# A decoder trunk on one core: two of three units in step at the stage entries, low parts moved on VectorE, and a retention end with three open output tiles

## The reference

```
for i in range(4):
    a = rms_norm(h, norm_g[i, 0])
    m = gmlp(a) if i % 3 == 0 else nsa(a) if i % 3 == 1 else retention(a)
    h = h + rms_norm(m, norm_g[i, 1])
    f = (silu(b @ w_gate) * (b @ w_up)) @ w_down      # b = rms_norm(h, norm_g[i, 2])
    h = h + rms_norm(f, norm_g[i, 3])
```

## Time and profile before

| | us |
|---|---|
| median of 3 runs | 2926.41 |
| profiled execution, its own time | 2926.34 |
| its span, first to last instruction | 2924.6 |
| TensorE busy, of the span | 2848.6 (97%) |
| VectorE, ScalarE, GpSimd busy | 1382.0, 978.5, 479.6 |
| high part of one unit on ScalarE, mean of 461 | 1.05 |
| mean granted TensorE clock, of full speed | 0.993 |

### The profile page before, as it was taken

The page is one execution under the profiler, slowest core; times in us unless marked ns, Lnnn a source line. Parts: engine busy times, 40 slices in busy tenths (PEclk is TensorE's granted clock), DMA queues, the critical chain, the costliest instruction groups (busy, mean ns, idle before and its releaser), DMA issues. The chain is left out here.

```text
span 2924.6 us, 37780 instructions
## 1 busy us (share of the span) xinstructions
PE 2848.6 (97%) x14556; PEld 2348.3 (80%) x14556; DVE 1382.0 (47%) x1827; ACT 978.5 (33%) x1563; POOL 479.6 (16%) x371
## 2 busy tenths in 40 slices
PE   7999999999999999999999997999999999999998
PEld 5888888888876688888877775888888788888887
DVE  3464543335667654333544555443334365443333
ACT  4332432225254443222422232333223333332222
POOL 0021122201101212220011211022210012022210
PEclk9999999999999999999999998999999999999999
DMA  4323233334410023333322221233332323233331
GB/s 147 92 81 94 73 101 100 99 98 120 132 53 2 16 72 108 93 99 100 98 83 79 72 86 51 73 107 94 91 100 83 112 84 90 76 101 93 99 98 56
DMA packets 459669, 256.07 MB, mean 88 GB/s; under 512 B 9632, under 2 KB 447632, under 8 KB 459424
## 3 DMA queue, kind: packets, MB, share of 16 engines
q1 hardware_dynamic: 457792, 249.65, 29.3%
q10 hardware_dynamic: 1152, 2.62, 0.3%
q0 software_dynamic: 608, 2.16, 0.2%
HBM read 248.11 MB, written 2.10 MB: 86 GB/s over the span
## 5 line engine op out<-in xcount | busy, mean ns | idle before, releaser
L1447 DVE TENSOR_TENSOR w_lo<-w_raw,w_hi 128x1024 fp32r<-128x1024 f32 x461 | 626.6, 1361 | 887.5 <-ACT w_hi L1071 887.2
L493 PE MATMUL acc<-a_hi,w_hi 128*128 128x512 f32 x2264 | 889.0, 393 | 6.9 <-DVE y_lo L1906 5.1
L495 PE MATMUL acc<-a_hi,w_lo 128*128 128x512 f32 x2264 | 879.5, 388 | 0.0
L494 PE MATMUL acc<-a_lo,w_hi 128*128 128x512 f32 x2072 | 806.4, 389 | 0.0
L1071 ACT ACTIVATE w_hi<-w_raw 128x1024 fp32r<-128x1024 f32 x461 | 483.4, 1050 | 515.3 <-PE acc L495 510.4
L493 PEld LDWEIGHTS acc<-a_hi,w_hi 128*128 128x128 f32 x2264 | 425.8, 188 | 99.3 <-issue 12.8
L495 PEld LDWEIGHTS acc<-a_hi,w_lo 128*128 128x128 f32 x2264 | 425.3, 188 | 87.7
L494 PEld LDWEIGHTS acc<-a_lo,w_hi 128*128 128x128 f32 x2072 | 389.2, 188 | 80.1 <-issue 1.4
L495 PE MATMUL acc<-hid_hi,w_lo 128*128 128x512 f32 (+1 forms) x704 | 264.5, 376 | 0.0
L494 PE MATMUL acc<-hid_lo,w_hi 128*128 128x512 f32 (+1 forms) x704 | 264.5, 376 | 0.0
L493 PE MATMUL acc<-hid_hi,w_hi 128*128 128x512 f32 (+1 forms) x704 | 264.5, 376 | 0.0
(11 more groups left out here) (303 smaller groups left out, 3465.7 us busy)
## 6 DMA issues: line engine op xcount, KB each, us to landing
w_raw<-ffn_w_gate SPq DMA_DIRECT2D x88, 512.0 KB, 3.8
w_raw<-ffn_w_up SPq DMA_DIRECT2D x88, 512.0 KB, 3.8
w_raw<-gm_w_in SPq DMA_DIRECT2D x64, 512.0 KB, 4.1
w_raw<-ffn_w_down SPq DMA_DIRECT2D x64, 512.0 KB, 3.8
w_raw<-ret_w_in SPq DMA_DIRECT2D x48, 512.0 KB, 3.7
w_raw<-gm_w_out SPq DMA_DIRECT2D x32, 512.0 KB, 3.9
w_raw<-ffn_w_down SPq DMA_DIRECT2D x32, 384.0 KB, 3.3
w_raw<-nsa_w_in SPq DMA_DIRECT2D x21, 512.0 KB, 4.0
```

The costliest lines, as they stand in the source:

```text
L493: pe.matmul(o_bank, lhs_hi, rhs_hi, start=start, stop=False)
L494: pe.matmul(o_bank, lhs_hi, rhs_lo, start=False, stop=False)
L495: return pe.matmul(o_bank, lhs_lo, rhs_hi, start=False, stop=stop)
L1447: dve.tensor_tensor(w_lo[:, slot, :, :], w_raw[:, slot, :, :], w_hi[:, slot, :, :].bitcast(f32), ALU.subtract).then_inc(lo_done, 1)
```

## The change

It has four parts.

1. In `entry`, the third unit is left out of tiles k = 0 and 1 of half 0, and its 12 matmuls for these two tiles are made up after k = 1. Nothing else is added; each wait stands before the first matmul that needs it.
2. In VectorE's boundary, the third unit's low part goes from step 2 to step 3, the reading of the old tile's second half (`last_tile(1)`) from step 3 to step 4 (at boundaries 6 and 8 too), and the fourth unit's low part from step 5 of half 0 to behind both halves (not at boundary 6, nor 0).
3. In the last retention head, VectorE makes y_lo 0 to 7 in pairs ahead of the four copies of `ro`, then centres, makes y_lo 8 to 11, and then the low parts of output units 3 and 4 (counted from 0), which before stood in the residual code behind y_lo 15. ScalarE makes their high parts earlier too.
4. TensorE starts the output product before `norm_mean`, and keeps three output tiles open: unit 0 (split around `norm_mean`), unit 2, the first half of unit 1, `norm_var`, the first half of unit 3, unit 4, and only then the second halves of units 1 and 3, which need y tiles 12 to 15.

```diff
+                def products(hf, k, of):
+                    pe.wait_ge(a_hi_done, step_of(b, hf, k))
+                    for j in of:
+                        slot, bank = units[j]
+                        if hf == 0 and k == 0:
+                            pe.wait_ge(lo_done, n0 + j + 1)
+                        pe.matmul(acc[:, bank, half(hf)], w_hi[:, slot, k, :], a_hi[:, k, half(hf)], start=k == 0, stop=False)
+                        pe.matmul(acc[:, bank, half(hf)], w_lo[:, slot, k, :], a_hi[:, k, half(hf)], start=False, stop=False)
+                    pe.wait_ge(a_lo_done, step_of(b, hf, k))
...
+                        products(hf, k, range(ENTRY - 1 if hf == 0 and k < 2 else ENTRY))
+                        if hf == 0 and k == 1:
+                            products(0, 0, [ENTRY - 1])
+                            products(0, 1, [ENTRY - 1])
...
+                def part(j, k0, k1, then=0):
+                    n, o, t = L["n_out"] + j, L["o_out"] + j // 2, j % 2
+                    pe.wait_ge(lo_done, n + 1)
+                    if t == 0:
+                        wait(pe, acc_free, o - BANKS + 1)
+                    for k in range(k0, k1):
+                        kk = t * KMAX + k
+                        pe.wait_ge(y_lo_done, kk + 1)
...
+                part(0, 0, 6)
                 norm_mean(RH)
-                def last_var(i, j):
-                    if isinstance(i, int) and i == 0 and j == 0:
-                        norm_var(RH)
-                dense(L["n_out"], L["o_out"], 2, 8, TWO, y_hi, y_lo, after=last_var, operand=(y_lo_done, 0), tail_of=L["b_mid"])
+                part(0, 6, 8, then=1)
+                part(2, 0, 8)
+                part(1, 0, 4)
+                norm_var(RH)
+                part(3, 0, 4)
+                part(4, 0, 8)
+                part(1, 4, 8, then=2)
+                part(3, 4, 8, then=2)
+                dense(L["n_out"], L["o_out"], 2, 8, TWO, y_hi, y_lo, begun=5, tail_of=L["b_mid"])
...
# ScalarE, end of retention
                     split_y(0, 8)
+                    split_unit(L["n_out"] + AHEAD)
                     act.wait_ge(rs_done, 4 * RH)
                     split_y(8, 12)
                     squares(RH)
+                    split_unit(L["n_out"] + AHEAD + 1)
...
# VectorE, boundary
-                            if step == 2 and G >= 2:
+                            if step == 3 and G >= 2:
                                 split_unit(n0 + 2)
-                            if step == 3:
+                            if step == 4:
                                 last_tile(1)
...
-                        if step == 5 and hf == 0:
+                        if step == 5 and hf == 0 and (last or into_gmlp(b)):
                             split_unit(n0 + AHEAD)
...
                 if not into_gmlp(b):
+                    split_unit(n0 + AHEAD)
                     split_unit(n0 + AHEAD + 1)
...
# VectorE, end of retention
                         for e in range(4):
+                            if isinstance(i, int) and i == RH - 1:
+                                split_y(2 * e, 2 * e + 2)
                             dve.wait_ge(ro_done, i * 4 + (e + 1))
...
-                    loop(dve, RH, head, 1)
+                    loop(dve, RH, head, 1, 1)
                     centre(RH)
-                    split_y(0, 8)
+                    split_y(8, 12)
+                    split_unit(L["n_out"] + AHEAD)
+                    split_unit(L["n_out"] + AHEAD + 1)
                     variance(RH)
-                    split_y(8, 12)
                     finish_head(RH)
                     split_y(12, 16)
```

More of the change, by code:

```diff
@@ L389, in step_bank @@
             return st[:, :, :] if s % 2 == 0 else acc[:, 1:3, :]
+        OUT_BEGUN = [L["n_out"] for L in PL if L["kind"] == 2]
         block = ctx.enter_context(nc.Block())
@@ L501, in entry @@
                 wait(pe, acc_free, o0 + ENTRY - BANKS)
+                def products(hf, k, of):
[7 more added lines that the diff above has]
+                    pe.wait_ge(a_lo_done, step_of(b, hf, k))
+                    for j in of:
+                        slot, bank = units[j]
+                        last = pe.matmul(acc[:, bank, half(hf)], w_hi[:, slot, k, :], a_lo[:, k, half(hf)], start=False, stop=k == DT - 1)
+                        if hf == 1 and k == DT - 1:
+                            last.then_inc(unit_done, 1)
                 for hf in range(2):
                     for k in range(DT):
-                        pe.wait_ge(a_hi_done, step_of(b, hf, k))
-                        for j, (slot, bank) in enumerate(units):
-                            if hf == 0 and k == 0:
-                                pe.wait_ge(lo_done, n0 + j + 1)
-                            pe.matmul(acc[:, bank, half(hf)], w_hi[:, slot, k, :], a_hi[:, k, half(hf)], start=k == 0, stop=False)
-                            pe.matmul(acc[:, bank, half(hf)], w_lo[:, slot, k, :], a_hi[:, k, half(hf)], start=False, stop=False)
-                        pe.wait_ge(a_lo_done, step_of(b, hf, k))
-                        for slot, bank in units:
-                            last = pe.matmul(acc[:, bank, half(hf)], w_hi[:, slot, k, :], a_lo[:, k, half(hf)], start=False, stop=k == DT - 1)
-                            if hf == 1 and k == DT - 1:
-                                last.then_inc(unit_done, 1)
+                        products(hf, k, range(ENTRY - 1 if hf == 0 and k < 2 else ENTRY))
+                        if hf == 0 and k == 1:
+                            products(0, 0, [ENTRY - 1])
+                            products(0, 1, [ENTRY - 1])
                         if k % 4 == 3:
@@ L1019, in retention @@
                 loop(pe, RH, head, 1)
-                norm_mean(RH)
-                def last_var(i, j):
-                    if isinstance(i, int) and i == 0 and j == 0:
-                        norm_var(RH)
-                dense(L["n_out"], L["o_out"], 2, 8, TWO, y_hi, y_lo, after=last_var, operand=(y_lo_done, 0), tail_of=L["b_mid"])
+                def part(j, k0, k1, then=0):
[6 more added lines that the diff above has]
+                        pe.wait_ge(y_lo_done, kk + 1)
+                        last = product(acc[:, o % BANKS, :], w_hi[:, n % SLOTS, k, :], w_lo[:, n % SLOTS, k, :], tile(y_hi, kk), y_lo[:, kk, :],
+                                       kk == 0, kk == 2 * KMAX - 1)
+                    if then:
+                        last.then_inc(unit_done, then)
+                part(0, 0, 6)
+                norm_mean(RH)
+                part(0, 6, 8, then=1)
[7 more added lines that the diff above has]
+                dense(L["n_out"], L["o_out"], 2, 8, TWO, y_hi, y_lo, begun=5, tail_of=L["b_mid"])
             pe.wait_ge(params, 16)
@@ L1100, in residual @@
                     for j in range(t * G, t * G + G):
-                        split_unit(n0 + j + AHEAD)
+                        if t or n0 not in OUT_BEGUN:
+                            split_unit(n0 + j + AHEAD)
                     act.wait_ge(unit_done, n0 + t * G + G)
```

3 lines of the change are left out of this document (2 added, 1 removed).

## The result

The changed kernel takes 2895.09 us (median of 4 runs, 2893.8 to 2898.89), the one before 2926.52 in the same rounds. The ratio is 0.9896, with a 95% interval of 0.9882 to 0.991. Predicted were 2895.0, in a range of 2888 to 2906. The profiled execution took 2895.1 us with a span of 2893.4. In the later rounds one execution of e1 took 5777 us and one of the kernel before 7276; both are left out of the ratios.

A forecast was written before the change was run, and what follows sets the result against it. TensorE, busy 97% of the span, was taken as the bound, with gains only in its waits, lower clock or the end. Boundaries 14.9 plus retention's end 16.3 made 31.2 off 2926.34: 2895 us, range 2888 to 2906.

The forecast's parts named there:

- Entries: Boundaries 1, 2, 4, 5, 7, first matmul with the third unit to `f_roots`: 2.5 us gained each, 12.5 together.
- TensorE has 12 matmuls behind it, not 4: Entries: when the third unit's low part comes, TensorE has done 12 matmuls instead of 4, with 51 to go.
- Half 1 hangs on `f_roots` at 695.12, and `f_roots` on TensorE's place in its own program: Entry of boundary 2: claimed that whatever TensorE gains by `f_roots` it keeps.
- Rival B: Entries bound by VectorE and ScalarE, not TensorE's place: 7.5 us less gained, 2902.5 us; chance 0.11.
- The clock cost nothing there and gives nothing back: Entries 1 and 7: half clock for 3.4 us after a 1.74 wait, yet the same 10.26 us to `f_roots`.
- Rival C: Clock falls after the remaining 0.8 us waits: 1.1 lost at three entries, boundary 3's gain gone, 2899 us; chance 0.07.
- The cover: Entries: the moved fourth unit's low part still ends 1.4 us before TensorE needs it, so it costs nothing.
- one of three reasons for late a_lo: Entries: third unit's low part, a 0.75 us stall before the old tile, and fourth unit's low part (1.23) delay a_lo.
- Boundary 3, 6, 8: Gains outside the five entries: 0.7 us at boundary 3, 1.0 at boundary 6, 0.7 at boundary 8.
- Retention: Retention's end: unit 4's place passed at 1797.8, not 1814.1, gaining 16.3 us (12 to 20).
- rival A: Last head: GpSimd loses the port too, six sums each held up 0.6 us by a y_lo: 2898.5 us; chance 0.11.
- Rival D: Slower: weights arrive late, as the eighth unit's load hangs on the fourth's low part at six entries: 2932 us; chance 0.02.

The follow-up runs named there:

- e1: Kernel before with only TensorE's new entry order (part 1 of the change): 2926.7 us, ratio 0.9999.
- e2: Kernel before with only VectorE's new order at the boundaries (part 2 of the change): 2918.7 us, ratio 0.9968.
- e3: Kernel before with both new orders at the boundaries (parts 1 and 2), retention's end unchanged: 2915.14 us, ratio 0.9958.
- e4: Kernel before with only the changed end of retention (parts 3 and 4): 2910.35 us, ratio 0.9948.
- e11: Kernel of e2 with 12 idle matmuls in TensorE's wait for the third unit's low part at entries 1, 5 and 7: 2913.63 us.
- e6: Changed kernel with two further VectorE subtractions ahead of the fourth unit's low part at six boundaries: 2903.48 us.
- e5: Changed kernel with the fourth unit's low part put back to step 5 of half 0: 2895.51 us.
- e9: Changed kernel with 14 idle matmuls on TensorE ahead of the entry at boundary 3: 2894.01 us.
- e10: Changed kernel with the last head's finish reordered: product with the reciprocal last, tile by tile, each tile's y_hi and y_lo following at once: 2891.14 us.
- e12: Changed kernel with the edits of e9 and e10, plus third-tile a_hi matmuls ahead of the made-up unit at entries 1, 5, 7: 2889.99 us, ratio 0.9876.
- e8: Changed kernel with the low part of output unit 4's weights made after the variance's scaling, not before: 2895.21 us.

## Why the prediction was right, and where it was not

**Entries.** The size was right (2.5 against 2.45), and so was the measure (7.8 from the low part to `f_roots`, 7.73 found). The argument "TensorE has 12 matmuls behind it, not 4" explains a quarter of it. What failed is the step "Half 1 hangs on `f_roots` at 695.12, and `f_roots` on TensorE's place in its own program": TensorE's place alone gives 0.0 (e1), VectorE's order alone 1.89 (e2), and only on top of this is TensorE's worth 0.56 (e3). The sum came out because it counted all idle time of the stretch as recoverable, having checked separately that VectorE keeps up after the edit; it never asked how much each would give without the other. Rival B, that VectorE binds, had the right engine and the wrong price, since the same edit moves VectorE.

**The clock.** "The clock cost nothing there and gives nothing back" is true of the kernel before and of e4, where it falls at entries 1 and 5 with no loss. (Before, the entries of boundaries 1 and 7, with a fall, take 12.64 and 12.65 us to `f_roots`, that of boundary 5, where the clock stayed up, 12.66.) It is no rule: with VectorE early the same half clock costs 1.50 (e2 against e11). The change avoids this only since its other part shortens the wait to 0.87. Rival C feared a fall there; it came at none of the 24 waits of 0.87 in eight profiles.

**The fourth low part.** The cover was 1.47 (1.4 predicted) and proved by e6. But the forecast named this subtraction as one of three reasons for late a_lo, and there e5 finds 0.07. That leaves the other two, the third unit's low part a step later and the old tile's second half without its stall. This is argued and not shown: e5 was made with TensorE's new order in place, not with its old one as in e2, and the two moves were not parted.

**Boundary 3, 6, 8.** 0.27 against 0.7: the clock fell again, and e9 puts its price at 1.0. Boundary 6 was undersized (1.60 against 1.0): only the longest of four waits was counted, and the printed waits went down from 1.5 to 0.3. Boundary 8 was right.

**Retention.** 15.42 against 16.3; e4 gives 15.32 alone, so the two halves of the change add up. The steps came at the places foreseen: no wait at `norm_mean` and `norm_var`, one for y_lo of 4.05 (4.3), unit 5's low part late by 0.40 (0.2). The term mis-sized was the clock: the 12 matmuls behind the wait take 5.04 us (1782.46 to 1787.50), 2.3 over the 2.74 of the full pace, not 1.7. The prediction took it that the loss shrinks with the wait. It hardly does: it was 2.5 behind 8.60. The clock's 0.6 and unit 5's 0.2, less 0.25 for the shorter wait, are 0.55 of the missing 0.9; the rest is within the scatter of the stretch.

Of the port, which was rival A: a y_lo beside a running GpSimd sum took 1.7 us of VectorE's time in place of 0.6, a w_lo 2.2 in place of 1.15. GpSimd loses as well, but only what is left of the subtraction that it meets. In the changed kernel's last head five sums started with 0.27 to 0.44 us of a VectorE subtraction still to go and took 1.50 to 1.64; the sixth met none and took 1.29. Where more is left, more is lost. In an earlier head of the kernel before, a sum starts 0.17 us behind a low part:

```profile
1515.43 1.21 DVE L1447 TENSOR_TENSOR w_lo<-w_raw,w_hi 128x1024 fp32r<-128x1024 f32 x1
...
1515.60 2.19 POOL L2020 TENSOR_TENSOR SS<-SS,ro 128x512 f32<-128x512 f32 x1 [0.89 <-DVE ro L1900]
```

So the mechanism of rival A is there, and its price of 0.6 a sum isn't, since in the last head the sums come late in a y_lo. The Trainium skill, "SBUF — State Buffer", section "SBUF: two separate sides", has whoever starts first hold the pair for the whole instruction; these rows agree for both engines. Rival D is out too: no wait for the fourth unit or a later one of an entry is in the trace.

## What to carry to other kernels

When two engines take turns in a chain, idle time counted on one of them is a ceiling for both edits together; ask what each gives alone, and expect the waits to change names when only one moves. Price a wait of TensorE with the clock that follows it, and look again at a half clock that "costs nothing" once the engine that hid it gets faster. Where the wait can't be filled with work, a dozen idle matmuls into a bank about to be overwritten paid for themselves here.

## What the runs showed of the hardware

The clock's answer to a wait is not certain. Behind waits of TensorE of 1.74 us in entries 1, 5 and 7 it fell 7 times in 9 (kernel before, e2, e4), behind 2.15 in e1 3 in 3, behind 1.89 in entry 3 11 in 12, behind 3.69 to 4.05 for y_lo 7 in 7. Behind 0.87 it never fell in 24, nor behind waits of 1.3 to 1.5 among matmuls of 512 columns in 21 (those of e10 and e12 are two of them).

The length of the wait doesn't decide alone. At the last boundary, where a wait of 1.26 is followed by one of 1.72 or 2.44, the clock fell in all 14 profiles. In the attention stage it fell behind a wait of 1.89 in 4 of 14, behind one of 1.25 in 2 (e1, e8), and in 3 (e2, e6, e8) with no printed wait, behind 48 matmuls of 64 and 31 columns. In e8:

```profile
800.09 1.89 PE L820 MATMUL tr<-w,h1v 128*128 128x64 f32 x16
801.91 2.02 PE L831 MATMUL st<-kcr,nq 64*128 64x31 f32 x32
...
803.80:807.00 3.20, 3.20 (x12) 2.65 (x12) 2.02 (x3) 3.10 (x6) 0.94 (x1) 0.50 1.09 265
```

These nine falls lie in six executions, and only there did the stage lose time: 1.65 to 2.28 with one fall (e1, e4, e5), 3.20 and 4.02 with two (e8, e2). Whether they also make the spread between executions without a trace is not shown. In the entries, what a fall cost depended on TensorE being the late one: nothing at entry 1 before, 1.50 in e2. The Trainium skill, "TensorE: Matmul & The Clock Gate", section "Why this matters for your kernels", warns of gaps between bursts of matmuls; in kind the traces agree, but gaps of 1.7 to 1.9 us, shorter than those it names, sufficed here.

A reciprocal on VectorE takes 3.35 us for 128 x 512, a multiplication of the same size 0.6 to 0.7 (changed kernel, lines 1889, 1893 and 1897). The Trainium skill, "VectorE: DVE Perf Modes", section "First, the fixed hardware budget", says that it is an iterative divide; here it stands in the one chain that TensorE still waits for.
